# Decays of a gated delta rule from loaded rows of cumulative sums, and a second attention in another order of TensorE's queue

## The reference

```python
def chunk_gated_delta(q, k, v, g, beta):
    ...
    g = jnp.cumsum(g.reshape(bsz, nh, nc, CHUNK), axis=-1)
    lower = jnp.tril(jnp.ones((CHUNK, CHUNK), dtype=bool))
    strict = jnp.tril(jnp.ones((CHUNK, CHUNK), dtype=bool), -1)
    gdiff = g[..., :, None] - g[..., None, :]
    decay = jnp.where(lower, jnp.exp(jnp.where(lower, gdiff, 0.0)), 0.0)
    L = jnp.where(strict, jnp.einsum('bhncd,bhnmd->bhncm', kb, k) * decay, 0.0)
    ...
    T = lax.linalg.triangular_solve(eye + L, ...)
    ...
    qk = jnp.where(lower, jnp.einsum('bhncd,bhnmd->bhncm', q, k) * decay, 0.0)
    def step(state, inp):
        v_new = u_c - jnp.einsum('bhcd,bhde->bhce', w_c, state)
        o = (jnp.einsum('bhcd,bhde->bhce', q_c * jnp.exp(g_c)[..., None], state)
             + jnp.einsum('bhcm,bhme->bhce', qk_c, v_new))
        ...
# one layer of the first block (2 layers)
proj = rmsnorm(x, norm_w[l]) @ w_in[l]
y_a = gated_delta_branch(...)      # the delta rule forwards and backwards in time, 8 heads
y_b = diff_attention_branch(...)
x = x + (sigmoid(gate_a) * (y_a @ w_pa[l]) + sigmoid(gate_b) * (y_b @ w_pb[l])) @ w_out[l]
# one layer of the second block (2 layers): sliding-window, decayed (mLSTM) and
# forgetting attention side by side, an output projection, a feed-forward part
s = jnp.where(allowed, q @ k.T / 8, -inf);  p = softmax(s);  o = p @ v
```

## Time and profile before

| | |
|---|---|
| median of 3 runs | 3366.11 us (3365.68 to 3367.87) |
| the profiled execution | 3367.48 us, its span 3365.7 us |
| mean granted TensorE clock | 0.974 of full |
| PE busy | 3133.6 us (93%) |
| PEld, DVE, ACT busy | 2452.7, 1687.5, 1466.4 us |
| POOL busy | 418.3 us (12%) |
| DMA | 225.17 MB, mean 67 GB/s |

### The profile page before, as it was taken

How to read it: one execution, slowest core, us unless ns; L and a number is a source line. 1 busy time by engine, 2 the same in 40 slices (tenths; PEclk the granted TensorE clock), 3 DMA queues, 4 the chain that set the end, 5 groups by cost and what they waited for, 6 DMA issues and landing times. The chain is left out here.

```text
span 3365.7 us, 55961 instructions
## 1 busy us (share of the span) xinstructions
PE 3133.6 (93%) x22464; PEld 2452.7 (73%) x22464; DVE 1687.5 (50%) x2498; ACT 1466.4 (44%) x2848; POOL 418.3 (12%) x276
## 2 busy tenths in 40 slices
PE   6999979999899999889998989889999899899998
PEld 4777767777776777767776857767888667678887
DVE  6666642566446666633665334444333444544333
ACT  4444532465333454433555244643333345543332
POOL 1434420000013444300000010001000000010000
PEclk9999999999999999999999989989999999999999
DMA  3111104322331111023222333103333231033332
GB/s 107 51 39 39 39 8 107 77 71 54 85 82 51 45 33 52 14 68 86 66 68 52 102 75 79 38 19 109 98 93 94 75 82 38 26 85 92 99 100 75
DMA packets 377886, 225.17 MB, mean 67 GB/s; under 512 B 25536, under 2 KB 357824, under 8 KB 377152
## 3 DMA queue, kind: packets, MB, share of 16 engines
q1 hardware_dynamic: 377664, 222.06, 24.4%
HBM read 214.68 MB, written 2.10 MB: 64 GB/s over the span
## 5 line engine op out<-in xcount | busy, mean ns | idle before, releaser
L313 PE MATMUL bank<-hT,ws 128*128 128x512 f32 x2144 | 909.6, 424 | 61.3 <-DVE hT L462 31.4
L317 PE MATMUL bank<-hT,ws 128*128 128x512 f32 x2144 | 846.4, 395 | 0.0
L316 PE MATMUL bank<-hT,ws 128*128 128x512 f32 x2144 | 845.0, 394 | 0.0
L313 PEld LDWEIGHTS bank<-hT,ws 128*128 128x128 f32 x2144 | 408.1, 190 | 178.7 <-issue 90.5
L267 DVE TENSOR_TENSOR ws<-raw,ws 128x2048 fp32r<-128x2048 f32 x164 | 376.8, 2298 | 250.2 <-ACT ws L261 247.0
L261 ACT ACTIVATE ws<-raw 128x2048 fp32r<-128x2048 f32 x176 | 336.5, 1912 | 331.3 <-PE bank L313 196.7
L317 PEld LDWEIGHTS bank<-hT,ws 128*128 128x128 f32 x2144 | 407.0, 190 | 89.8
L316 PEld LDWEIGHTS bank<-hT,ws 128*128 128x128 f32 x2144 | 409.1, 191 | 83.2 <-issue 13.9
L874 PE MATMUL bank<-uS,ws 128*128 128x512 f32 x512 | 201.8, 394 | 0.0
L878 PE MATMUL bank<-uS,ws 128*128 128x512 f32 x512 | 201.2, 393 | 0.0
L877 PE MATMUL bank<-uS,ws 128*128 128x512 f32 x512 | 200.3, 391 | 0.0
(11 more groups left out here) (355 smaller groups left out, 4981.4 us busy)
## 6 DMA issues: line engine op xcount, KB each, us to landing
raw<-in_w_in SPq DMA_DIRECT2D x196, 512.0 KB, 4.6
raw<-in_w_ff SPq DMA_DIRECT2D x128, 512.0 KB, 4.5
raw<-in_w_out SPq DMA_DIRECT2D x32, 512.0 KB, 5.5
raw<-in_w_pa SPq DMA_DIRECT2D x16, 512.0 KB, 5.5
raw<-in_w_pb SPq DMA_DIRECT2D x16, 512.0 KB, 5.4
raw<-in_w_in SPq DMA_DIRECT2D x16, 256.0 KB, 4.2
sq<-rq SPq DMA_DIRECT2D x48, 64.0 KB, 2.1
xT<-in_xT SPq DMA_DIRECT2D x1, 2048.0 KB, 7.8
```

The source lines that it names most:

```text
L313: first = pe.matmul(out, hi, x[:, 0, k], start=(begin and k == steps[0]), stop=False)
L316: pe.matmul(out, hi, x[:, 1, k], start=False, stop=False)
L317: last = pe.matmul(out, lo, x[:, 0, k], start=False, stop=(end and k == steps[-1]))
```

## The change

Delta phase. The cumulative sums of all heads, once made, are turned on TensorE (one plain-fp32 matmul with the identity, `turn_sums`), copied by ScalarE (`copy_rows`) and stored as 64 rows of 128 numbers in DRAM (`sum_rows`). For each head SyncE loads its eight rows, each broadcast to all 128 partitions (512 KB), twice: into `rows` (`load_rows`, which takes the place of gU) and into qte (`load_query_rows`). Both matmul groups, `decay_args` and `decay_rows`, are gone, and with them three uses of the scratch bank in a head. The table's column QG now holds the cumulative sum of a token. `decay_terms` subtracts that column from the rows, for the forward direction into Ec and for the backward one into EB. VectorE cuts both at 0 from above and adds them (`cut` in level 2, `arguments` in level 3). The cut replaces the mask: on the wrong side of the diagonal a difference is positive and becomes 0. ScalarE takes the exponential in place (`decay_exp`), and one exponential of 128x1024 over qte (`row_exp`, in level 1) instead of two of 128x512. GpSimd's `decay_terms` goes ahead of `k_decay`, and `beta_decay` waits for `arguments`. VectorE's convolution instructions are spread anew. SyncE's loop is written out by hand, with the row loads between the weight loads.

Second attention. The values product of a unit is issued one unit later, right behind the turning of the next unit's weights; all five fill steps stand at the end of a unit. ScalarE's `scale_out` goes behind the copy AT, and the reciprocals get a ring of four (`inv`).

```diff
+    def turn_sums(self, pe):
+        pe.wait_ge(self.e_in, 2)
+        pe.transpose(self.RT, self.u[:, 0].rearrange("p d x -> p (d x)"), self.k.ident).then_inc(self.turned, 1)
+
+    def copy_rows(self, act):
+        act.wait_ge(self.turned, 1)
+        act.activation(self.rt[0:64], self.RT, ACT.Copy).then_inc(self.rows_copied, 1)
+
+    def store_rows(self, sp):
+        sp.wait_ge(self.rows_copied, 1)
+        sp.dma_start(self.k.sum_rows, self.rt[0:64]).then_inc(self.rows_stored, 16)
+        sp.wait_ge(self.rows_stored, 16)
...
     def act_decays(self, act):
         act.wait_ge(self.e_in, 2)
+        act.wait_ge(self.turned, 1)
...
-            chain(dve.tensor_copy(T[:, QG, d], self.g[:, d]))
 
     def dve_third(self, dve, chain):
         u = self.u
         dve.wait_ge(self.sums, 2)
         chain(dve.tensor_copy(u[:, 0], self.SUMS))
+        for d in range(2):
+            chain(dve.tensor_copy(self.T[:, QG, d], u[:, 0, d].rearrange("p (c h) -> p c h", h=HEADS)))
...
                     pool.wait_ge(hc_ready, h + 1)
-                    for d in range(2):
-                        pool.tensor_tensor(gU[:, d], per_chunk(upto(d)), per_token(hc[:, p, QG, d * NS:(d + 1) * NS]),
-                                           ALU.mult).then_inc(gu_ready, 1)
+                    pool.wait_ge(rows_in, 16 * (h + 1))
+                    if h > 0:
+                        pool.wait_ge(kqc_ready, h)
+                    for d, out in enumerate((Ec, EB)):
+                        pool.tensor_tensor(out[:, :, :], rows[:, d], per_token(hc[:, p, QG, d * NS:(d + 1) * NS]),
+                                           ALU.subtract).then_inc(terms_ready, 1)
 
...
-                    pool.wait_ge(x_taken, scratch_use("gb", core) + 1)
+                    pool.wait_ge(qexp_ready, h + 1)
...
                     inverse_start(i)
+                    if ahead:
+                        decay_terms(i + 1, 1 - p)
                     k_decay(i, p, i - 1)
                     q_decay(i, p, i)
-                    if ahead:
-                        decay_terms(i + 1, 1 - p)
                     kq_masks(i)
...
+                def head_rows(h):
+                    return k.sum_rows.rearrange("(d c h) n -> h d c n", d=2, h=HEADS)[h].rearrange("d c n -> (d c) n").unsqueeze(0).broadcast_to([P, 2 * NS, P])
+
+                def load_rows(h):
+
+                    if h > 0:
+                        sp.wait_ge(terms_ready, 2 * h)
+                    sp.dma_start(rows.rearrange("p d c n -> p (d c) n"), head_rows(h)).then_inc(rows_in, 16)
+
+                def load_query_rows(h):
+
+                    if h > 0:
+                        sp.wait_ge(o_done, h)
+                    sp.dma_start(qte.rearrange("p d (c n) -> p (d c) n", n=P), head_rows(h)).then_inc(qrows_in, 16)
+
+                def refill(h, c):
+                    st.taken(sp, h, c)
+                    if h + 1 < HEADS:
+                        st.load(sp, h + 1, c)
+                    else:
+                        following.load(sp, 0, c)
+                refill(0, 0)
+                refill(0, 1)
+                gates.store_rows(sp)
+                load_rows(0)
+                load_query_rows(0)
+                refill(1, 0)
+                load_rows(1)
+                refill(1, 1)
+                for h in range(HEADS):
+                    if h > 0:
+                        load_query_rows(h)
+                    if h + 2 < HEADS:
+                        refill(h + 2, 0)
+                        load_rows(h + 2)
+                        refill(h + 2, 1)
...
-                def decay_args(h, core):
-                    pe.wait_ge(gu_ready, nth(h, 2, 1))
-                    scratch("arg", core)
-                    for d in range(2):
-                        last = pe.matmul(B[XB][:, :], strict(1 - d), gU[:, d].rearrange("p c n -> p (c n)"), start=(d == 0), stop=(d == 1))
-                    last.then_inc(x_ready, 1)
-
-                def decay_rows(h, d, core):
-                    pe.wait_ge(gu_ready, nth(h, 2, d))
-                    scratch(("gf", "gb")[d], core)
-                    pe.matmul(B[XB][:, :], k.ones, gU[:, d].rearrange("p c n -> p (c n)"), start=True, stop=True).then_inc(x_ready, 1)
...
-                        if a < 2:
-                            decay_rows(i, a, i)
                         if a == 2 and not first:
                             turn_out(i - 1, i)
-                        if a == 3 and ahead:
-                            decay_args(i + 1, i)
                         if a == 4:
                             turn_v(i, i)
...
-                def decay_exp(h, core):
-                    act.wait_ge(x_ready, scratch_use("arg", core) + 1)
-                    if h > 0:
-                        act.wait_ge(kqc_ready, h)
-                    act.activation(Ec[:, :, :], b4(B[XB]), ACT.Exp).then_inc(x_taken, 1)
-
-                def row_exp(h, d, core, first):
-                    act.wait_ge(x_ready, scratch_use(("gf", "gb")[d], core) + 1)
-                    if not first:
-                        act.wait_ge(o_done, h)
-                    act.activation(qte[:, d], B[XB][:, :], ACT.Exp).then_inc(x_taken, 1)
+                def decay_exp(h):
+                    act.wait_ge(arg_ready, h + 1)
+                    act.activation(Ec[:, :, :], Ec[:, :, :], ACT.Exp).then_inc(ec_ready, 1)
+
+                def row_exp(h):
+                    act.wait_ge(qrows_in, 16 * (h + 1))
+                    act.activation(qte[:, :, :], qte[:, :, :], ACT.Exp).then_inc(qexp_ready, 1)
...
+                def cut(h):
+
+                    dve.wait_ge(terms_ready, 2 * h + 1)
+                    dve.tensor_scalar(Ec[:, :, :], Ec[:, :, :], 0.0, None, ALU.min).then_inc(arg_step, 1)
+
+                def arguments(h):
+
+                    dve.wait_ge(terms_ready, 2 * h + 2)
+                    dve.wait_ge(arg_step, h + 1)
+                    dve.scalar_tensor_tensor(Ec[:, :, :], EB[:, :, :], 0.0, Ec[:, :, :], ALU.min, ALU.add).then_inc(arg_ready, 1)
...
+                                cut(i + 1)
+                            some(fill, 1)
+                        elif a == 3:
+                            if ahead:
+                                arguments(i + 1)
                             some(fill, 2)
-                        elif a == 3:
-                            some(fill, 3)
                         else:
                             some(fill, 1)
...
+                            some(fill, 3)
...
+                def values(u):
+                    T, m, kind, n = unit(u)
+                    ks = keys(kind, n)
+                    if u == FIRST_UNIT[m]:
+                        pe.wait_ge(vtm_ready, m + 1)
+                    pe.wait_ge(at_ready, u + 1)
+                    if u > 0:
+                        pe.wait_ge(scaled, 2 * u)
+                    for h in range(2):
+                        for y, kb in enumerate(ks):
+                            last = pe.matmul(B[OB][:, n * P + 64 * h:n * P + 64 * h + 64], AT[:, u % 2, h, y * P:(y + 1) * P],
+                                             vtm[:, m % 2, kb, 64 * h:64 * h + 64], start=(y == 0), stop=(y == len(ks) - 1))
+                    last.then_inc(pv_ready, 1)
...
-                    some(fill, QUOTA // 2 + 1)
                     if kind == MLSTM:
...
+                        values(u - 1)
                     for mj in due(u, "turn"):
                         turn_v(*mj)
                     if n == out_turn(T - 1):
                         turn_out(T - 1)
-                    some(fill, QUOTA - QUOTA // 2 - 1)
-                    if u == FIRST_UNIT[m]:
-                        pe.wait_ge(vtm_ready, m + 1)
-                    pe.wait_ge(at_ready, u + 1)
-                    if u >= NTOK:
-                        pe.wait_ge(scaled, 2 * (u - NTOK + 1))
...
+                    some(fill, QUOTA)
+                values(UNITS - 1)
...
                     act.activation(AT[:, u % 2, :, 0:w], ps[:, TB:TB + 2, 0:w], ACT.Copy).then_inc(at_ready, 1)
+                    if u > 0:
+                        scale_out(u - 1)
...
-                    if u >= 2:
-                        dve.wait_ge(scaled, 2 * (u - 1))
-                    dve.reciprocal(s[:, 4:6], s[:, 2:4]).then_inc(r_ready, 1)
+                    if u >= 4:
+                        dve.wait_ge(scaled, 2 * (u - 3))
+                    dve.reciprocal(inv[:, u % 4], s[:, 2:4]).then_inc(r_ready, 1)
```

More of the change, by code:

```diff
@@ L978, in __init__ @@
             "exp_ready", "lambda_exp")
+        self.turned, self.rows_copied, self.rows_stored = k.sems("sums_turned", "sum_rows_copied", "sum_rows_stored")
         self.W = 4 * HEADS
@@ L1088 @@
 INNER = LEVELS - 2
-X_HEAD0 = ("k", "ss", "arg")
-X_CORE0 = ("gf", "gb", "arg", "v", "k", "ss")
-X_CORE = ("gf", "gb", "o", "arg", "v", "k", "ss")
-X_LAST = ("gf", "gb", "o", "v", "out")
+X_HEAD0 = ("k", "ss")
+X_CORE0 = ("v", "k", "ss")
+X_CORE = ("o", "v", "k", "ss")
+X_LAST = ("o", "v", "out")
```

(29 more changed lines are left out.)

25 lines of the change are left out of this document (16 added, 9 removed).

## The result

The changed kernel takes 3346.45 us (median of 5 runs, 3338.32 to 3354.79), the kernel before 3366.11: a ratio of 0.9942, 95% interval 0.9929 to 0.9956. It is 20 us faster, not 57, and lies outside the predicted range. Its own runs differ by 16 us; those of before by 3.4. The profiled execution is the slowest of them, 3354.79 us with a span of 3353.0.

A forecast was written before the change was run, and what follows sets the result against it. TensorE's queue bounds the delta phases (busy 47.92 of 50 us); the second attention is looser, with waits. Gains of 38 (delta) and 19 (attention) make 57: 3367.5 - 57 = 3310.5, as a median 3309; 8 in 10 range 3284 to 3333.

The forecast's parts named there:

- The row loads cost nothing: Delta phase: 512 KB row loads land in time, like a weight piece in 4.6 us, and cost nothing.
- Rival D: Delta phase: query rows come late and the kernel is slower, 3394 at a landing of 31 us; chance 0.02.
- A with B: VectorE sets the delta levels and the attention's order only exchanges waits, together 3347; chance 0.05.
- The matmuls' price: Delta phase: each removed row matmul costs 0.85 us, 32 of them 27.2 us a layer.
- Rival E: Delta phase: the removed matmuls were hidden, so only the attention's gain counts, 3347; chance 0.04.
- The charge of 0.6 us a core for VectorE: Delta cores: late VectorE instructions lose 0.3 in the levels and 0.3 in the recurrence; bounds 0 and 1.6.
- Rival A: Delta levels: VectorE's three-instruction groups beside GpSimd set the level, delta gain only 19, 3328; chance 0.12.
- Before head 0: Delta phase start: TensorE stands 2.8 us for a late `pad_copy`, charged 1.5 a layer, between 0 and 3.
- 12 of 19 us: Second attention: fewer TensorE waits gain net 9.7 a layer, 19 for both; bounds -6 to 34.
- clock term: Second attention: the clock stays up where waits were, a gain of 3 us a layer.
- that term of 1.2: Second attention: the wait for turned v falls by 0.4 in each of three places, 1.2 a layer.
- Rival B: Second attention: the new order only exchanges waits, 0 net, 3328; chance 0.15.

The follow-up runs named there:

- e_pitch: Changed kernel with each stored row of sums widened to 576 bytes, so a load's pieces lie 4608 B apart, not 4096: 3309.36 us, ratio 0.9836.
- e_bload: Kernel before plus 32 unneeded 512 KB loads to a DRAM scratch area at the places of the row loads: 3445.26 us, ratio 1.0222.
- e_tiny: Changed kernel with both row loads of heads 1 to 7 cut to 16 elements a partition: 3311.27 us, ratio 0.9833.
- e_delta: Kernel before with only the delta-phase part of the change, its attention left as it was: 3358.29 us, ratio 0.9967.
- e_first: Changed kernel with each decay row load asked for before the weight piece beside it: 3349.74 us, ratio 0.9946.
- e_half: Changed kernel with only the query rows of heads 1 to 7 cut to 16 elements a partition: 3347.18 us, ratio 0.9942.
- e_wide: Changed kernel with sums stored head by head in 512 B pieces, 4096 B from row to row: 3330.57 us, ratio 0.9891.
- e_attn: Kernel before with only the second attention's part of the change: 3356.05 us, ratio 0.9964.
- e_mm: e_start plus four unread plain-fp32 128x512 matmuls a core in levels 0 and 1: 3357.83 us, ratio 0.9974.
- e_start: Changed kernel with sums stored head by head (4 KB pieces) and ScalarE's first exponentials not waiting for the turning: 3304.88 us, ratio 0.9809.
- e_kilo: Changed kernel with sums stored head by head in 512 B pieces, 1024 B from row to row: 3313.94 us.
- e_pad: Changed kernel with sums stored head by head in 512 B pieces, 576 bytes from row to row: 3311.59 us, ratio 0.9832.

## Why the prediction was wrong

**The row loads cost nothing: this step failed.** I asked only whether the rows would land in time for those who wait for them. Rival D did too. They did, but for one wait of GpSimd: 2.8 us, in a core of 50.6 us (head 0 of layer 1). The price was paid by a transfer that no line of the kernel asks for, the packets of TensorE's instructions. The bytes were judged by weight pieces in 4.6 us and one broadcast in 9.1; the 9.1 was the nearer row, and I did not ask why 256 KB took twice as long as 512. The stops and the clock behind them cost about 42 us in the profiled execution; by medians, `e_pitch` without them is 37 us faster, as much as the gap between forecast and result. That slow row loads cause the stops is shown by adding and by taking away (`e_bload`, `e_tiny`, `e_pitch`). That the late instruction packet is the link is read from the traces: six kernels (changed, `e_delta`, `e_first`, `e_half`, `e_wide`, `e_bload`) have 44 stops in their cores, and every one ends 1.27 to 1.55 us behind the end of a q8 packet. No run tested it by itself, and what a slow load does to the fetching of a packet is not shown.

**What is left is partly luck.** `e_pitch` took 3309.36, and the forecast was 3309, but its other terms were wrong too and happen to cancel: VectorE's charge was about 12 us too high over 14 cores, while the attention gave 7 us less than forecast by `e_attn`, and the start of head 0 cost some 7 more, if layer 1 lost the 5.3 of layer 0. The measured 3346 lies within 1 us of A with B and of E (3347), by chance: their mechanisms are not there.

**The matmuls' price was right.** `e_mm` gives 53 for 54. Rival E is out.

**The charge of 0.6 us a core for VectorE was too high.** Most clean cores are 3.6 to 3.8 us shorter, not 2.8. The matmuls alone are 3.4, so VectorE took nothing that shows. Rival A is out: in `e_start` TensorE is busy 47.58 of 50 us in mid-phase, nearly as in the earlier trace rows, and no wait for Q stands in its list:

```profile
170.00:220.00 50.00, 47.58 (x731) 38.47 (x731) 35.41 (x55) 25.89 (x65) 22.93 (x15) 1.00 0.23 65
```

`cut` and `arguments` took 0.98 and 1.04 us in the median of 16, not the 1.51 and 1.43 of the earlier trace rows. They do run beside GpSimd. Its timeline, and VectorE's at the same time:

```profile
207.12 2.53 POOL L1246 TENSOR_TENSOR qte<-cb,qte 128x512 f32<-128x512 f32 x2 [4.90 <-ACT qte L1604]
209.61 3.16 POOL L1257 TENSOR_TENSOR kqm<-Nn,cg 128x512 f32<-128x512 f32 x2
```

```profile
208.97 0.97 DVE L1796 TENSOR_SCALAR Ec<-Ec 128x512 f32<-128x512 f32 x1 [0.16 <-DVE tmv L1778]
209.85 1.77 DVE L1749 SCALAR_TENSOR_TENSOR cb<-cb,cw 128x512 f32<-128x512 f32 x1
```

The cut ended 0.3 us behind GpSimd's q products, the multiply-add after it took 1.77 us, and TensorE shows no wait for Q behind them.

**Before head 0 the mechanism was right and the size wrong.** 2.8 us came, but I let slack take half of it and left out the clock: 5.3 us late in layer 0, not 1.5. `e_start` shows both parts gone with the one wait.

**The attention gave 12 of 19 us, and its clock term had the wrong sign.** In thirteen profiles with the new order it takes 218.7 to 224.6 us from scores to last values, and in three with the old one (before, `e_delta`, `e_bload`) 222.2 to 228.3. In layer 0 the waits for fill tiles fell from 4.4 and 1.3 to 1.1 us and none, AT's 2.0 went, the 5.4 became 1.6; masked weights cost 2.0 and qk's first scores 3.0 where it was 1.9. The wait for turned v stayed at 4.9: that term of 1.2 was wrong. Rival B, no gain at all, is out. Waits of TensorE, changed kernel, 2032 to 2275 us:

```profile
PE bank L2619 <- ACT vtm L2746: 4.9, 3, 2.3
...
PE bank L2631 <- DVE qk L2876: 3.0, 1, 3.0
...
PE bank L2690 <- ACT Sm L2758: 2.0, 3, 1.4
...
PE bank L313 <- issue: 1.6, 1, 1.6
```

Behind the 3.0 the clock falls, and stays down:

```profile
2224.00:2237.00 13.00, 11.44 (x48) 8.83 (x48) 5.45 (x8) 6.97 (x19) 0.00 (x0) 0.50 0.00 0
```

The forecast took 3 us a layer back from the clock. In fact TensorE was granted 1.2 GHz for 27.3 and 34.1 us of the two attentions, before for 23.9 and 20.5: half of the difference is 1.7 and 6.8 us lost. Where the new order had 20.5 us at 1.2 GHz too (eight stretches, of `e_tiny`, `e_kilo` and `e_pitch` among others), it took 218.7 to 220.1 us against the 227.0 of before. So at equal clock it gives 7 to 8 us a layer, close to the 6.7 that the forecast had without its clock term. Over 2685 to 2960 us the granted clock is 0.93, before it was 0.95. Two things stand behind the 1.6 in place of 5.4: the turning, the values and a turned output now come ahead of that wait, and they run at 1.2 GHz. In layer 1 of `e_mm`, where TensorE was at full clock for the 5 us before that wait, it is 2.8; so part of it was paid in clock instead.

**A page's rule, weighed.** Packets of 512 B moved mostly at 150 to 300 GB/s in `e_pitch` and at about 85 in `e_wide`, so their size did not make the difference here. The Trainium skill ("Perfetto Trace Analysis", section "DMA Optimizations") says that DMAs under 2 KB have significant overhead each. Taken of packets, that rule would make `e_pad` and `e_pitch` as slow as the changed kernel, and they were not; their query rows landed in 4.2 us, against 3.7 with 4 KB pieces.

## What to carry to other kernels

A transfer added to a quiet part of a kernel has two prices: whether its reader waits, and what it does to those who share the queues, the loading of instructions among them. Such stops show as "issue" in the middle of a group of equal instructions, and the DMA view of the time before them shows no packet of the instruction queue. Where a scratch layout puts pieces 4096 B apart, a wider row is a cheap thing to try first; here it gave 37 us. And waits of TensorE like those read here, of 2.4 to 3.9 us, are to be priced with the half clock behind them, here half as much to as much again.

## What the hardware showed that was not expected

- Reading eight pieces of 512 B for each of 128 partitions from one small area took 8.3 us with 4096 B from piece to piece, 4.2 with 4608 or 576, 3.9 with 1024, and 3.7 in one piece of 4 KB. Why 4096 is special is open.
- TensorE resumed 1.27 to 1.55 us after a late instruction packet had landed, in all 44 stops of six kernels. A packet held 256 of its instructions.
- In the changed kernel, stops of 2.4 to 3.9 us made a core 4.2 to 6.4 us longer than the clean 49.7 of other kernels.
